# Decode attention inside the prompt attention's pipeline, a narrower bias table, a streamed compression and a shorter routing

## The reference, cut to what matters

```
p, u, v, q, kv, gates = split_proj(h @ w_in)      # pooling, gating, attention inputs
kvc = compress(cmp_raw, cmp_pe, cmp_w1, cmp_w2)   # per 32 tokens: gelu((x + pe) @ w1) @ w2, k and v, per group
# nsa_core, for every query:
s_c = q . kc  * scale + tb[rel_bucket(dist_c)];   p_c = masked_softmax(s_c, dist_c >= 0)
s_s = q . k_s * scale + tb[rel_bucket(dist_s)];   p_s = masked_softmax(s_s, dist_s >= 0)
s_w = q . kw  * scale + tb[rel_bucket(dist_w)];   p_w = masked_softmax(s_w, window of 512)
out = gates[0] * (p_c @ vc) + gates[1] * (p_s @ v_s) + gates[2] * (p_w @ vw)
# rel_bucket is constant from a distance of 128 on
# prompt: keys are the prompt's; decode: 256 cached rows (through a page table, or a window buffer) + 8 new ones
x = layer_norm(ALPHA * x + (1 + g1) * (mix @ w_out));  h2 = x * (1 + sc2) + sh2
s = sigmoid(h2 @ router_w)       # best of 4 groups, 2 best of its 4 experts, weights s / sum
# tokens sorted by expert, each expert's list padded to blocks of 128
y[e] = (silu(x_blk @ w_gate[e]) * (x_blk @ w_up[e])) @ w_down[e]
x = layer_norm(ALPHA * x + (1 + g2) * ff)
```

## Time and profile before

| | |
|---|---|
| median of 3 runs | 1498.45 us (1494.69 to 1502.95) |
| profiled execution | 1498.93 us, span 1496.8 us |
| busy PE, DVE, ACT, POOL | 1282.4, 742.0, 528.9, 108.5 us |
| projection | 0 to 395.6 us |
| compression | 395.6 to 471.3 us |
| decode attention | 471.3 to 535.0 us |
| prompt attention | 535.0 to 810 us |
| output projection and routing | 810 to 983 us |
| experts and combination | 983 to 1496.8 us |

### The profile page before, as it was taken

One profiled execution on the slowest core, in us unless ns is written; L12 is line 12 of the kernel. 1 busy time (PEld: TensorE's weight loads), 2 busy tenths in 40 slices (PEclk: granted clock), 3 DMA queues, 4 the chain that ended last, 5 costly groups with the idle time before them and its releaser, 6 DMA issues. The chain is left out here.

```text
span 1496.8 us, 21480 instructions
## 1 busy us (share of the span) xinstructions
PE 1282.4 (86%) x7890; PEld 929.3 (62%) x7891; DVE 742.0 (50%) x1547; ACT 528.9 (35%) x873; POOL 108.5 (7%) x159
## 2 busy tenths in 40 slices
PE   4289999999538989999997999279999999999962
PEld 1156666665326556656666887167788887788731
DVE  0012222221212545656676666768856658675248
ACT  0010000100000137755555221157646457665132
POOL 1000011000000000000000000001101001110040
PEclk9599999999757559999999999569999999999986
DMA  9753345500432063000003332559976769975572
GB/s 328 237 162 137 134 162 90 97 12 12 100 88 81 14 213 126 2 1 1 2 2 103 112 118 106 191 185 371 375 261 240 268 245 362 376 248 207 204 285 94
DMA packets 100626, 237.69 MB, mean 159 GB/s; under 512 B 19914, under 2 KB 27525, under 8 KB 100391
## 3 DMA queue, kind: packets, MB, share of 16 engines
q1 hardware_dynamic: 88951, 196.47, 39.3%
q0 software_dynamic: 8144, 27.62, 5.1%
q10 hardware_dynamic: 3456, 12.58, 2.1%
HBM read 198.61 MB, written 40.13 MB: 159 GB/s over the span
## 5 line engine op out<-in xcount | busy, mean ns | idle before, releaser
L2079 PE MATMUL psum<-w_hi,x_parts 128*128 128x512 f32 x736 | 240.3, 398 | 8.4 <-DVE x_parts L2198 7.5
L2191 DVE TENSOR_TENSOR w_lo<-raw,w_hi 128x2048 fp32r<-128x2048 f32 x96 | 215.6, 2288 | 56.8 <-ACT w_hi L2138 56.7
L2138 ACT CAST w_hi<-raw 128x2048 fp32r<-128x2048 f32 x96 | 178.5, 1912 | 93.5 <-DVE work L2209 50.6
L592 PE MATMUL psum<-low,high 128*128 128x512 f32 (+5 forms) x576 | 200.3, 502 | 0.0
L2079 PEld LDWEIGHTS psum<-w_hi,x_parts 128*128 128x128 f32 x736 | 139.9, 190 | 39.9 <-issue 11.0
L592 PEld LDWEIGHTS psum<-low,high 128*128 128x128 f32 (+1 forms) x576 | 105.4, 188 | 77.5 <-issue 66.9
L2079 PE MATMUL psum<-w_lo,x_parts 128*128 128x512 f32 x368 | 144.6, 393 | 0.0
L1501 DVE CUSTOM_DVE_ANT_0 low<-psum,high 128x512 f32<-128x512 f32 (+3 forms) x160 | 88.8, 593 | 78.1 <-PE psum L1341 77.8
L2079 PE MATMUL psum<-w_hi,a_parts 128*128 x368 | 121.2, 401 | 5.6 <-DVE a_parts L2204 5.5
L1469 ACT ACTIVATE low<-low,high 128x640 f32<-128x640 f32 (+7 forms) x128 | 93.0, 729 | 51.4 <-DVE high L1501 51.4
L1664 PE MATMUL psum<-wo_parts,mix_parts 128*128 128x512 f32 (+1 forms) x432 | 104.0, 398 | 6.8 <-DVE wo_parts L1801 6.2
(11 more groups left out here) (310 smaller groups left out, 1519.9 us busy)
## 6 DMA issues: line engine op xcount, KB each, us to landing
raw<-in_moe_w_gate SPq DMA_DIRECT2D x16, 2048.0 KB, 11.2
raw<-in_moe_w_up SPq DMA_DIRECT2D x16, 2048.0 KB, 12.0
raw<-in_moe_w_down SPq DMA_DIRECT2D x16, 2048.0 KB, 11.2
high<-in_w_mod SPq DMA_DIRECT2D x12, 2048.0 KB, 13.9
y_d<-work ACTq DMA_DIRECT2D x24, 512.0 KB, 7.0
high<-in_x_prompt SPq DMA_DIRECT2D x16, 512.0 KB, 3.9
y_d<-high SPq DMA_DIRECT2D x1, 8192.0 KB, 37.3
low<-in_w_in SPq DMA_DIRECT2D x3, 2048.0 KB, 15.1
```

The costliest lines, as they stand in the source:

```text
L592: mm = pe.matmul(c.bank(2 + n % 2)[0:T, 0:w], hT[i % 2][:, k, 0:T], c.w_in[:, k, a:a + w], start=(k == 0), stop=(k == KT - 1))
L2079: mm = pe.matmul(out, left[l][:, k * P:(k + 1) * P], w[:, bass.ds(at + k * step, 512)], start=n == 0, stop=n == len(steps) - 1)
L2138: act.copy(c.w_hi[:, at:at + PART // 2], c.raw[:, o:o + PART // 2]).then_inc(hi_done[p], 1)
L2191: dve.tensor_tensor(c.w_lo[:, at:at + PART // 2], c.raw[:, o:o + PART // 2], c.w_hi[:, at:at + PART // 2].bitcast(F32), ALU.subtract).then ...
```

## The change

- The bias table keeps the 512 nearest columns; farther ones are all equal, and are read as column 0 by broadcast. The compressed branch has a table of its own, made by two DVE copies.
- Compression: eight buffers, contiguous loads of 2 KB per row (one DMA per prompt tile, one per page), a copy on ACT that puts the pairs in order, `w1` and `w2` issued on ACT's queue at the start, and `xcT` laid out so that each product reads adjacent columns.
- The block of the decode attention is gone. Its bias sums come at steps 1 and 2 of the prompt pipeline, its gates at step 3, its transposed keys two groups a step at steps 6, 7, 14 and 15, and six items (a branch and a half, both key groups) after the pairs 9, 11, ..., 19, that is at steps 10, 13, ..., 25. SP loads their keys first; the fill of `y_d` and `w_out` follow.
- Routing: unlinked instructions where nothing depends on them, tables in bf16, tile sums by nine products instead of a chain of additions, one-hot tables in four instructions, the weights moved to the end, two DMAs for the constants.

```diff
-                src = bass.AP(tensor=c.tab_d.tensor, ..., ap=[[TABW - 1, TROWS], [TROWS * TABW, NH], [1, D]])
+                src = bass.AP(tensor=c.tab_d.tensor, ..., ap=[[TABW - 1, TROWS], [TROWS * TABW, NH], [1, NEAR]])      # NEAR = 512
 # block_compression, SP
-                if n >= 3:
-                    sp.wait_ge(nt_ps, n - 2)
+                if n >= NAT:
+                    sp.wait_ge(paired, n - NAT + 1)
-                        for q in range(2):
-                            sp.dma_start(dst[64 * pg:64 * pg + 64, :, q, :], src[:, q]).then_inc(nat_in[n % 3], 16)
-                if n == 3:
-                    sp.dma_start(w1, ...)
-                    sp.dma_start(w2, ...)
+                        sp.dma_start(dst[64 * pg:64 * pg + 64, :], src).then_inc(nat_in[n % NAT], 16)
 # PE
-                    cols = xcT[:, 2 * s:2 * s + 2, :].rearrange("p g (n c) -> p g n c", c=CB // 2)[:, :, :, k]
-                    mm = pe.matmul(..., w1[:, s, k, :], cols, ...)
+                    mm = pe.matmul(c.bank(2 + s)[:, 0:2 * nblk], w1[:, s, k, :], xcT[:, s, k, :], ...)
 # ACT
+            act.dma_start(w2, ...)
+            act.dma_start(w1, ...)
+            for n in range(tiles):
+                act.wait_ge(nat_in[n % NAT], need[n])
+                if n >= 2:
+                    act.wait_ge(nt_ps, n - 1)
+                act.copy(pairs[n % 2], nat[n % NAT].rearrange("p q a d -> p a q d")).then_inc(paired, 1)
 # DVE
-                            xcT[:, 2 * s + g, n * P:(n + 1) * P].rearrange("p (n c) -> p n c", c=CB // 2),
-                            c.bank(n % 2)[...].rearrange("p (n c) -> p n c", c=CB // 2),
+                            xcT[:, s, :, g * nblk + 8 * n:g * nblk + 8 * n + 8],
+                            c.bank(n % 2)[...].rearrange("p (n c) -> p c n", c=CB // 2),
 # block_prompt_attention
+    SAMPLE = [(br, half) for br in (2, 1, 0) for half in range(2)]
+    for p in range(NPAIR):
+        order.append(("prompt", p))
+        if p >= SAMPLE_FROM and (p - SAMPLE_FROM) % 2 == 0 and (p - SAMPLE_FROM) // 2 < len(SAMPLE):   # SAMPLE_FROM = 9
+            order.append(("sample", (p - SAMPLE_FROM) // 2))
+    first_key_step = {2: place["sample", 0] - 4, 1: place["sample", 1] + 1}
 # SP
+            sp.dma_start(nat_win, t["state_win_kv"]...)
+            for at in range(NB * NPAGE): ... sp.dma_start(nat_sel[:, at, :], ...)
+            sp.wait_ge(c.bias_in, 16 * (P // TROWS))
+            sp.dma_start(c.y_d[first:]...)
+            values_done(sp, place["sample", 3])
             sp.dma_start(c.w_out[:, 0:4, :], ...)
 # PE, at each step
+                if n in (1, 2):
+                    sample_bias(n - 1)
+                if n == 3:
+                    sample_gates()
+                for br, m in key_groups(n):
+                    sample_keys(br, m)
+                if n == out_step:
+                    sample_out()
 # GpSimd
+                    a = pool.tensor_copy(qs[...], c.qT[:, :, b:b + JS])      # x8
 # DVE: soft()
-                    bias = bias_w[:, h, :] if masked else c.bias[:, h, k:k + n * P]
+                    elif near < 0:
+                        bias = c.bias[:, 4 * g + j, 0:1].to_broadcast([P, cols])
+                    else:
+                        bias = c.bias[:, 4 * g + j, near:near + cols]
+            dve.tensor_copy(c.bias_c[:, :, 0:half_c], c.bias[:, :, 0:1].to_broadcast([P, NH, half_c]))
+            linked(dve.tensor_copy(c.bias_c[:, :, half_c:], c.bias[:, :, 31:512:32]))
 # block_routing, DVE
-            for i in range(NT):
-                tt(pref[:, i + 1], pref[:, i], tot[:, i], ALU.add)
+            linked(dve.tensor_reduce(totals, c.bank(1)[...].rearrange("p (i e) -> p e i", i=NT), AX.X, ALU.add))
-            for i in range(NT):
-                for k in range(2):
-                    dve.tensor_scalar(one_place[0:T, 2 * i + k], ..., ALU.is_equal)
-                    ins = dve.tensor_scalar(one_slot[0:T, 2 * i + k], ..., ALU.is_equal, ALU.mult)
+            tt(same_slot, slot_n..., slot_f..., ALU.is_equal)
+            dve.tensor_tensor(one_place, place_n..., place_f..., ALU.is_equal)
+            dve.tensor_scalar(one_slot[:, :, 0, :], same_slot, row, None, ALU.mult)
+            dve.tensor_tensor(one_slot[:, :, 1, :]..., same_slot..., tile_at..., ALU.mult).then_inc(dest_ready, 1)
 # block_routing, PE
+            pe.matmul(c.bank(1)[:, 0:NT * NE], ones_h, flat, start=True, stop=True).then_inc(cnt_ps, 1)
+            pe.matmul(c.bank(0)[:, 0:NT * NE], strict_h, flat, start=True, stop=False)
+            for n in range(1, NT):
+                mm = pe.matmul(c.bank(0)[:, 0:NT * NE], ones_h, padded[:, pad - n * NE:pad - n * NE + NT * NE], ...)
```

More of the change, by code:

```diff
@@ L1267, in pair, with blocks, pieces @@
         return i, br, j, k0, i + 1 - k0
-    def pieces(p):
-        i, br, j, k0, nk = pair(p)
+    def blocks(n):
+        kind, p = order[n]
+        if kind == "prompt":
+            return pair(p)[4]
+        return 3 if SAMPLE[p][0] else 1
+    def pieces(n):
+        nk = blocks(n)
         if nk <= 4:
@@ L1302, in turn_bank, with wait_read, last_turn, values_done @@
         return c.bank(4 + number[what] % 2)
-    def last_turn(p):
-        return number["pair", p, 1, (pair(p)[4] + 3) // 4 - 1]
+    def wait_read(eng, what):
+        n = number[what]
+        if by_act[n]:
+            eng.wait_ge(r_act, act_upto[n + 1])
+        else:
+            eng.wait_ge(r_dve, dve_upto[n + 1])
+    def last_turn(n):
+        return number["pair", n, 1, (blocks(n) + 3) // 4 - 1]
+    def values_done(eng, n):
+        if order[n][0] == "sample":
+            eng.wait_ge(t_ps, number["s_values", order[n][1]] + 1)
+        else:
+            eng.wait_ge(v_ps, sum(kind == "prompt" for kind, p in order[:n + 1]))
+    def keys_read(eng, br):
+        for m in (2, 3):
+            wait_read(eng, ("s_keys", br, m))
     with nc.Block() as block:
@@ L1343, in scores, with sample_scores @@
                 mm.then_inc(s_ps, 1)
-            def turn(p, g, n):
-                what = ("pair", p, g, n)
-                if n == 0:
-                    pe.wait_ge(e_ev, 2 * p + g + 1)
+            def sample_scores(n, q):
+                br, half = SAMPLE[order[n][1]]
+                if n == place["sample", 0]:
+                    pe.wait_ge(qs_ev, 1)
+                if br and half == 0:
+                    keys_read(pe, br)
+                for g in range(2):
+                    rows = slice(HD * g, HD * g + HD)
+                    left = qs[rows, half, :]
+                    out = c.bank(2 * g + q % 2)
+                    if br == 0:
+                        mm = pe.matmul(out[:, 0:NS], left, c.kcS[rows, NC_P:], start=True, stop=True)
+                        continue
+                    for b4 in range(4):
+                        pe.matmul(out[32 * b4:32 * b4 + 32, 0:PAST], left[:, 32 * b4:32 * b4 + 32], cache_kT[rows, 4 * half + b4, :],
+                                  start=True, stop=True)
+                    mm = pe.matmul(out[:, PAST:WK], left, c.kT[rows, br - 1, SEQ:], start=True, stop=True)
+                mm.then_inc(s_ps, 1)
@@ L1349, in turn @@
+            def turn(n, g, m):
+                what = ("pair", n, g, m)
+                if m == 0:
+                    pe.wait_ge(e_ev, 2 * n + g + 1)
                 bank_free(what)
-                for k in range(4 * n, min(4 * n + 4, pair(p)[4])):
-                    mm = pe.transpose(turn_bank(what)[:, (k - 4 * n) * P:(k - 4 * n + 1) * P], pb[p % 3][:, g, k * P:(k + 1) * P], c.ident)
+                for k in range(4 * m, min(4 * m + 4, blocks(n))):
+                    w = NS if order[n][0] == "sample" and k == blocks(n) - 1 else P
+                    mm = pe.transpose(turn_bank(what)[0:w, (k - 4 * m) * P:(k - 4 * m + 1) * P], pb[n % 3][:, g, k * P:k * P + w], c.ident)
@@ new lines, in turned @@
+            def turned(n):
+                if n >= 2:
+                    values_done(act, n - 2)
+                for g in range(2):
+                    what = ("pair", n, g, 0)
+                    act.wait_ge(t_ps, number[what] + 1)
+                    dst, src = pT[n % 2][:, g, :, :].rearrange("p k q -> p (k q)"), turn_bank(what)
+                    if order[n][0] == "prompt":
+                        w = min(4, blocks(n)) * P
+                        act.copy(dst[:, 0:w], src[:, 0:w]).then_inc(r_act, 1)
+                        continue
+                    w = (blocks(n) - 1) * P
+                    if w:
+                        act.copy(dst[:, 0:w], src[:, 0:w])
+                    act.copy(dst[0:NS, w:w + P], src[0:NS, w:w + P]).then_inc(r_act, 1)
@@ new lines, in sample_gates @@
+            def sample_gates():
+                what = ("s_gates",)
+                dve.wait_ge(t_ps, number[what] + 1)
+                for half in range(2):
+                    for g in range(2):
+                        linked(dve.tensor_tensor(gt, turn_bank(what)[:, 24 * half:24 * half + 24], rowm[:, g, :], ALU.mult))
```

(20 more changed lines are left out.)

831 lines of the change are left out of this document (420 added, 411 removed).

## The result

The changed kernel takes 1430.2 us (median of 4 runs, 1426.8 to 1433.1) against 1499.9 for the kernel before beside it: ratio 0.954, interval 0.950 to 0.9575. Forecast were 1429 us, 1408 to 1456. The profiled execution took 1433.1 us with a span of 1431.0, where that of before had 1496.8, so 65.8 us are to be found.

A forecast was written before the change was run, and what follows sets the result against it. Stage times add: cache DMA issue paces the stream, TensorE the attention, VectorE the routing. From 1498.9 us: -27.0 - 7.4 - 62.1 + 39 - 12.1 = -69.6, so 1429; range 1408 to 1456.

The forecast's parts named there:

- Compression stream: Compression loads: fewer, larger DMAs, w1 and w2 on ScalarE's queue; last add at 419.3 instead of 446.7, gain 27.0 us.
- the pages' issue: SyncE's queue in the compression stream: 16 cache pages at 1.05 us each, last issue at 414.8.
- Products: Compression's matmuls: contiguous moving operand instead of every sixteenth fp32 value, 13.7 against 21.1 us, gain 7.4.
- The decode block: Separate decode attention block between compression and prompt attention goes: gain 62.1 of its 64.2 us.
- The same work in the prompt pipeline: Decode work inside prompt attention: items, bias sums, keys, gates and copies add 39 us, nothing hidden by idle TensorE.
- Items and turn: Decode items in prompt attention: four at 3.7 us, two at 2, plus 1.8 for the result's turn; 20.6 us.
- Table of 512 columns: Bias table in prompt attention: DMAs shrink while TensorE is busy, far columns broadcast at the same length; no gain.
- Routing: Routing's VectorE chain: fewer waits, merged one-hots, shorter ids product and prefix work; gain 12.1 us, ends 8 and 15.
- (a): Prompt attention: decode work not overlapped, each item drains the pipeline, 39 becomes 62 us; 1452 us, chance 15%.
- (b): Prompt attention: decode work hides well and raises the clock early, 39 becomes 22 us; 1412 us, chance 12%.
- (c): Compression stream: no faster per byte, pages keep 2.1 us each, only 9 of 27 us saved; 1447 us, chance 7%.
- (d): Prompt attention: granted clock stays low, up to 180 us more, 1600 us, slower than before; chance 3%.

The follow-up runs named there:

- w1_after_4: Changed kernel with w1's 2 MB issued by ScalarE after the copy of tile 3 instead of ahead of tile 0: 1430.5 us.
- small_loads: Changed kernel with compression loads cut into 256-byte pieces as before, without ScalarE's copy, the eight buffers kept: 1452.0 us.
- two_queues: Changed kernel with the cache pages of compression tiles 5, 7, 9 and 11 loaded through GpSimd's queue instead of SyncE's: 1429.8 us.
- strided: Changed kernel with compression inputs stored as before, so the products read every 16th column: 1438.6 us.
- no_items: Changed kernel without the six decode items and the turn of their result, decode attention missing from the output: 1405.9 us.
- old_routing: Changed kernel with the routing block and constants of the kernel before: 1442.9 us.
- from33: Changed kernel with the decode items between prompt pairs 33 and 43 instead of from pair 9, key turns moved along: 1434.0 us.
- bias_late: Changed kernel with the decode bias sums moved from pipeline steps 1 and 2 to 8 and 9, gates from step 3 to 5: 1430.5 us.
- sums_in_stream: Changed kernel with the decode bias sums made during the compression stream instead of at prompt attention's steps 1 and 2: 1423.5 us.

## Why the prediction was right

The sum was -69.6 against a profiled 65.8. That the medians (1499.9 and 1430.2) differ by 69.7 is luck: the terms below are off by up to 4 us each, both ways. By its own steps:

1. Compression stream, forecast 27.0, measured 23.3 (51.0 us to 27.7). The mis-sized term is the pages' issue: 16 x 1.05 us by the decode pages of the earlier trace rows, against 16 x 1.19 here, and 1.5 us ahead of the first of them. The last issue ended at 419.1 instead of 414.8. From there to the last add it took 4.8 us where I had 4.5. w1, for which I had 10 us, took 19.7 beside the tiles (396.9 to 416.6) and held tiles 2 and 3 back to 405.6 and 407.6, but w1_after_4 shows that this did not set the end. small_loads shows that the gain is not the depth's, and by the price of an issue that it is their number's. What more could be won there stays open: with a second queue the bytes set the end (two_queues).
2. Products, forecast 7.4, measured 7.8; 0.165 us a record where I had 0.176. The Trainium skill's rule in "SBUF — State Buffer" (section "Door 1: The DMA port swizzle") that more than four fp32 of stride is penalised is borne out by strided; at the low clock no penalty is seen, 0.32 us either way. Its remark on non-contiguous PSUM speaks of matmuls; VectorE's strided reads took the same 0.22 us each as before.
3. The decode block, forecast 62.1, measured 62.4: between the last compression copy and the prompt block lay 64.2 us, now 1.8.
4. The same work in the prompt pipeline, forecast 39, measured 40.3. Items and turn 21.7 against 20.6 (no_items). Sums, gates, keys and the copies for bias_c 15.3 against 18.3: the sums 13.5 instead of 10, the gates 1.2 instead of 1.7, the window branch's keys 1.6 and the selected branch's 2.9 instead of 6 together, bias_c nothing seen instead of 0.6, and 3.7 won back between pairs 8 and 11 (no_items). That last term the forecast did not have: the sums fill a part of the low stretch, which is hardly longer for it (31.7 us against 29.8), so that pairs 7 to 10 come at the full clock. That this is the reason is read from the rows of the two kernels and not tested by itself. The dip adds 3.4, which the forecast did not have either. So errors of 3 to 4 us cancelled in this term, and its total was better than its parts, by luck. With small_loads' execution, which has the same attention code, the term would be 36.4.
5. Table of 512 columns, forecast nothing: from pair 20 to pair 63 attention takes 208.5 us against 209.0. No cost of the far columns' broadcast is seen. It was not run by itself.
6. Routing, forecast 12.1, measured 13.1 in the two traces and 12.7 by the medians of old_routing. The ids product ends at 913.8, before VectorE is done with the slot table (914.7), so it is hidden; the 2304-element one-hot took 2.56 us as estimated (1.1 ns an element).

Of the rivals, (a) and (b) fall with no_items, (c) with the stream's 27.7 us. (d) is the weak place of my text: I wrote that a fall of the clock between 500 and 740 us would show the forecast wrong. It fell, at 514.6, for 6.8 us, and cost an estimated 3.4. The sign should have been a length of some 95 us, as (d)'s own working had it. The Trainium skill's "TensorE: Matmul & The Clock Gate" (section "Loop structure matters more than you think") has the loop nest decide; here only the places of the items with their keys (from33) or of the sums and gates (bias_late) were changed, and the lasting rise moved from 31.7 us into the block to 45.5 and 46.9. Kernels with the changed kernel's attention code had the first rise at 26.4 to 31.7, so the two moves are clear of that.

## What to carry to other kernels

Moving a block's work into another block's pipeline is priced by the busy engine at the clock level of the steps where it lands, and not by its length alone: 62 us became 40 here, 13.5 of them for 11 us of products at the low clock, and what fills the low stretch can push the work behind it into the full clock (3.7 us back). Put such extra work where the busy engine waits for DMA (sums_in_stream, its two stages 10.6 us shorter together, the median 4 to 7), not merely later in the same dense stage. When a stream doesn't answer to an edit, follow the last tile: when it was issued, when it landed, when it was copied. In the changed kernel that shows the issue, in two_queues the bytes and a buffer, though both streams last 28 us.

## What the runs showed that I had not expected

- A dense stretch at the full clock can lose it: 6.8 us at the low level at 514.6, with TensorE busy in 38.3 of the 40.9 us ahead and never idle there for more than 0.8 us. Seven of the ten kernels with items from pair 9 fall once or twice, for 3.4 or 6.8 us, between 38 and 73 us into prompt attention; no_items and from33 don't, but small_loads doesn't either, with the same attention code as the changed kernel. What sets it stays open.
- Work moved from the low stretch to a later step can lengthen it (bias_late, from33), so that the time of a stage answers to the order of its first steps. It need not: with the sums out of the block altogether (sums_in_stream) the last rise ahead of the items stayed at 31.6 us, and the clock had been up for 13.7 us before.
- An issue of a cache page with its register load costs 1.05 us in the decode block (16 in 16.84 us of SyncE's queue), 1.19 in the stream of the changed kernel (16 in 19.06) and 1.13 in its prompt block (16 in 18.05). In the prompt block the instruction is that of the decode block, and 13 of the 15 distances are 1.10 us as there; the rest is in two, 1.91 and 1.48. In the stream, another instruction in another loop, every distance is 1.22 or more. What makes it dearer there stays open.
